# Constant products around the start of the attention, and the output stored in five transfers

## The chip, the cores and the metric

The kernel runs on one core of one Trainium2 chip. A core has four engines that compute: TensorE (PE in the profile) multiplies matrices into eight banks of 128 x 512 numbers, VectorE (DVE) and ScalarE (ACT) work elementwise, and GpSimd (POOL) here only issues gathers. SyncE (SP) issues transfers. Each engine runs its own list in order, and they wait for each other through semaphores. The metric is the device time of one execution in microseconds; less is better.

## What is computed

Two transformer layers on 512 rows of 1024 numbers, in 32-bit floats. What matters here are the attention of the first layer and the last product of the second:

```python
proj = jnp.einsum('bsd,de->bse', h, w_in)
(c_q, c_kv, k_r, q_b, k_b, v_b, q_i, k_i, w_i, g_a, g_b) = jnp.split(proj, splits, axis=-1)
...
o_a = chunk_causal_attention(q_a, k_a, v_a, (MLA_NOPE + MLA_ROPE) ** -0.5)
...
o_b = indexed_sparse_attention(q_b, k_b, v_b, q_i, k_i, w_i * (IDX_HEADS ** -0.5), top_k)
...
y = jax.nn.sigmoid(g_a) * y_a + jax.nn.sigmoid(g_b) * y_b
x = x + jnp.einsum('bsd,de->bse', y, w_out)
...
# second layer, its last stage: each row picks 128 of 16384 experts
act = jax.nn.gelu(jnp.einsum('chkd,cd->chk', u[ic], hc).astype(jnp.float32), approximate=False)
w = (gc * act).astype(h.dtype)
return jnp.einsum('chk,chkd->cd', w, v[ic])
```

Each of the two attentions has 8 heads and four blocks of 128 query rows; a block sees 512, 384, 256 or 128 keys. The sparse one masks all but the 128 best keys of a row, which a search with max and match_replace finds.

## The kernel before

The program is a row of blocks (`nc.Block()`). A block ends for all engines together: each goes on only when all have come to its end.

**The rows' stage** (the block of line 653) multiplies the normed rows with `w_in` in 40 pieces, each with a copy, a rotation and transposes behind it, and has the index search of the sparse attention beside it on VectorE (`dve_index`, lines 643 to 648). TensorE's list ends with a wait for the 24th index sum and `warm(e, 2, 7)` (line 706): two products of a constant matrix with a constant matrix into bank 7, which nobody reads. `warm` is the helper of lines 289 to 292; such products stand at eight more places of the program.

**The attention** (the block of line 825) runs two chains, `att_b` (sparse) and `att_a`, in steps, one head each a step, 32 heads and 7 more steps to drain. In step n TensorE does, for one chain and then for the other: the transposes of a finished block (line 401, few steps), the product of the weights with the values for head n - 5 (line 412, 64 columns each), the transposes of head n - 3 (line 421) and the product of queries and keys for head n (line 428). VectorE reduces that product (line 460), ScalarE takes the exponential (line 490), and the two take turns in copying the transposes (lines 451 and 481). The product for head n waits for the reduction of head n - 1 of its own chain, since both use the chain's one bank:

```python
if n:
    e.wait_ge(*(self.reduced if self.bias else self.powered)(n))
e.matmul(self.banks[0][:, 0:self.keys(i)], self.q(i, h), self.k(i, h), start=True, stop=True).then_inc(*self.scored.up(1))
```

The blocks with the most keys come first, so the first eight heads have 512 keys and the next eight 384. In the first three steps TensorE has nothing but the products of line 428. Bank 3, which belongs to chain b, is not used before the second block of query rows.

**The end** (the block of line 2512) multiplies gates with expert rows for row blocks 0 to 2 in 64 parts, `pe_second(e, n)`: part n is row group n // 2 and column half n % 2, and has for each row block `tb` twelve products into bank 2 * tb + n % 2 (lines 2505 to 2507). Each bank collects over all 32 groups. Row block 3 is worked out one row choice at a time by GpSimd's gathers and VectorE (`dve_row`, line 2153), the last of them at `r_used(256)`. When part 62 is done (`y_mm(63)`) VectorE adds the three banks of column half 0 to `X`, and when part 63 is done (`y_mm(64)`) those of column half 1 (line 2680). SyncE waits for the six additions and the row choices and stores all of `X` in one transfer (line 2554).

Of the kernel before, what the change touches and what calls it, by code (L numbers as in the profile page):

```python
# [175 lines left out]
def r(a):  # L176
    return a.bitcast(F32R)


def span(k, w=128):  # L180
    return slice(w * k, w * k + w)


def program(nc, d, out, sizes):
    ctx = ExitStack()
    with ctx:
# [4 lines left out]
        def sb2(name, shape, c):  # L191

            at = nc.sbuf_base
            a = sb(name, shape, c)
            assert at % 32 == 0 and nc.sbuf_base - at == 4 * int(np.prod(shape[1:]))
            t = nc.alloc_sbuf_tensor_at(name + "r", shape, F32, offset=at)
            return a, t[(slice(None),) * len(shape)]
# [3 lines left out]
        def sem(name, new=False):  # L201

            if new or not spare:
                s = Signal(ctx.enter_context(nc.semaphore(name)), 0)
            else:
                s = spare.pop(0)
            if not new:
                taken.append(s)
            return s
# [11 lines left out]
        X, XC = sb2("X", [128, 4, 1024], ctx)  # L221
# [31 lines left out]
        def wait_weight(e, n):  # L253
            e.wait_ge(*w_in[n % NS](16 * (n // NS) + 16))

        def weight(n):
            return W2[n % NS][0][:, 0:sizes[n]]
# [31 lines left out]
        def warm(e, times, bk, w=512):  # L289

            for _ in range(times):
                e.matmul(bank[bk][:, 0:w], ident, C[:, 0:w], start=True, stop=True)
# [207 lines left out]
        with ExitStack() as c0:  # L500
# [4 lines left out]
            with ExitStack() as c1:  # L505
                norm = Norm(c1, "mix", 0, 0, None, "mix")
                t_hi, t_lo = sems("t_hi t_lo")
                with nc.Block() as block:
                    @block.sync
                    def _(e):  # L510
                        e.dma_start(X, d["x"].rearrange("(b p) n -> p b n", p=128)).then_inc(*in_x.up(16))
                        e.dma_start(C, d["consts"]).then_inc(*in_c.up(16))
                        e.dma_start(G, d["gains"]).then_inc(*in_g.up(16))
                        load_weights(e, 3)
# [26 lines left out]
            with ExitStack() as c1:  # L541
# [111 lines left out]
                with nc.Block() as block:  # L653
# [4 lines left out]
                    @block.tensor  # L658
                    def _(e):
                        for step in range(45):  # L660
                            n = step
                            if n < 40:
                                t, tb = divmod(n, 4)
                                if tb == 0:
                                    wait_weight(e, t)
                                    if t in (6, 8):
                                        e.wait_ge(*r_keep(at[4 * (t - 6 if t == 6 else 5) + 3] + 1))
                                if n >= 2:
                                    e.wait_ge(*r_out(n - 1))
                                w, nw = weight(t), WIDTH[t]  # L670
                                bk = bank[n % 2][:, 0:nw]
                                if t < 6:
                                    hi, lo = RH[t % 2], W2[t % NS][1]
                                    for k in range(8):
                                        if tb == 0 and k % 2 == 0:
                                            e.wait_ge(*q_lo(4 * t + k // 2 + 1))
                                        a, c = span(tb), span(k, nw)
                                        e.matmul(bk, r(HTl[:, k, a]), r(hi[:, c]), start=k == 0, stop=False)
                                        e.matmul(bk, r(HTh[:, k, a]), r(lo[:, c]), start=False, stop=False)
                                        i = e.matmul(bk, r(HTh[:, k, a]), r(hi[:, c]), start=False, stop=k == 7)  # L680
                                else:
                                    lhs = cql if t < 8 else ckl
                                    for k in range(KK[t]):
                                        i = e.matmul(bk, lhs(k, tb), w[:, span(k, nw)], start=k == 0, stop=k == KK[t] - 1)
                                i.then_inc(*r_prod.up(1))
                            n = step - 4
                            if n in at:
                                t, tb = divmod(n, 4)
                                k = at[n]
                                e.wait_ge(*r_work(k + 1))  # L690
                                if k >= 2:
                                    e.wait_ge(*r_keep(k - 1))
                                s = SU[k % 4]
                                for g in range(2 if t == 8 else 1):
                                    bk = bank[2 + 2 * (k % 2) + g]
                                    p = 96 if t in (6, 7, 8) else 128
                                    srcs = [s[:, span(4 * g + j, p)] for j in range(2 if t == 5 else 4)]
                                    if t == 0:
                                        srcs[3] = kiN[:, tb, :]
                                    for j, x in enumerate(srcs):  # L700
                                        i = e.transpose(bk[0:p, span(j)], x, ident)
                                i.then_inc(*r_turn.up(1))
                            for u in index_units(step):
                                pe_logits(e, u)
                        e.wait_ge(*i_sum(24))
                        warm(e, 2, 7)

                    @block.scalar
                    def _(e):
# [115 lines left out]
                with nc.Block() as block:  # L825
                    @block.tensor
                    def _(e):
                        for step in range(att_b.steps()):
                            att_b.pe(e, step)
                            att_a.pe(e, step)  # L830

                    @block.vector
                    def _(e):
                        for step in range(att_b.steps()):
                            att_b.dve(e, step)
                            att_a.dve(e, step)

                    @block.scalar
                    def _(e):
                        for step in range(att_b.steps() + 1):  # L840
                            att_b.act(e, step)
                            att_a.act(e, step)
# [1233 lines left out]
        with ExitStack() as c0:  # L2076
# [90 lines left out]
            g_prod, g_hi, g_lo, v_hi, v_lo, y_mm, y_add = sems("g_prod g_hi g_lo v_hi v_lo y_mm y_add")  # L2167
# [51 lines left out]
            with ExitStack() as cx:  # L2219
# [247 lines left out]
                rows = lambda step: range(0 if step == 0 else round(turns[step - 1]), round(turns[step]))  # L2467
# [18 lines left out]
                    e.dma_start(AD[q // 4, :, q % 4, :], GA[q % 4]).then_inc(*ga_done[q % 4].up(16))  # L2486

                out_done = sem("out_done", True)

                def pe_second(e, n):  # L2490

                    g, c = n // 2, span(n % 2, 512)
                    gh, gl, vh, vl = GH[g % 2], GL[g % 2], VH[n % 3], VR[g % 2][1][:, :, c]
                    e.wait_ge(*g_lo(g + 1))
                    e.wait_ge(*v_lo(n + 1))
                    if n == 0:
                        e.wait_ge(*f_gelu(125))
                        e.wait_ge(*o_copy(96))
                    if n == 1:
                        e.wait_ge(*f_gelu(126))  # L2500
                        e.wait_ge(*c_ia(3))
                    for tb in range(3):
                        t, bk = span(tb), bank[2 * tb + n % 2]
                        for a in range(4):
                            e.matmul(bk, r(gl[:, a, t]), r(vh[:, a, :]), start=g == 0 and a == 0, stop=False)  # L2505
                            e.matmul(bk, r(gh[:, a, t]), r(vl[:, a, :]), start=False, stop=False)  # L2506
                            i = e.matmul(bk, r(gh[:, a, t]), r(vh[:, a, :]), start=False, stop=g == 31 and a == 3)  # L2507
                    i.then_inc(*y_mm.up(1))

                later = lambda n: range(ROWS1 + n * (256 - ROWS1) // 60, min(256, ROWS1 + (n + 1) * (256 - ROWS1) // 60))  # L2510

                with nc.Block() as block:
                    @block.sync
                    def _(e):
# [33 lines left out]
                        for k in range(2, 32):  # L2548
                            load_w(e, k)
                            load_a(e, k)  # L2550
                            load_v(e, k)
                        e.wait_ge(*y_add(6))
                        e.wait_ge(*r_used(256))
                        e.dma_start(out.rearrange("(b p) n -> p b n", p=128), X).then_inc(out_done.sem, 16)
                        e.wait_ge(out_done.sem, 16)

                    @block.gpsimd
                    def _(e):
# [71 lines left out]
                    def _(e):  # L2630
# [43 lines left out]
                            for q in later(n):  # L2674
                                dve_row(e, q)
                        for n in range(2):
                            e.wait_ge(*y_mm(63 + n))
                            for tb in range(3):
                                o = X[:, tb, span(n, 512)]
                                e.tensor_tensor(o, o, bank[2 * tb + n], ALU.add).then_inc(*y_add.up(1))  # L2680

# [16 lines left out]
```

## Time and profile before

| | us |
|---|---|
| median of 3 runs | 3118.2 |
| the runs | 3116.55, 3118.2, 3154.87 |
| device time of the profiled execution | 3154.56 |
| span of the profiled execution | 3152.7 |
| TensorE busy in it | 2977.3 (94%) |
| VectorE busy in it | 2002.0 (64%) |
| ScalarE busy in it | 1304.8 (41%) |
| mean granted TensorE clock, as a share of 2.4 GHz | 0.946 |

The span is the time from the first to the last instruction. The granted clock is what TensorE's throttle let through: 1.00 is 2.4 GHz and 0.50 is 1.2 GHz. A product of 32-bit numbers shows as two records. Matrix products are pipelined, and the end of a record is modelled: a record can reach into the next one, so the pace is read from start to start. Each row of a timeline merges like instructions that follow one another; "idle before" is the time in which that engine did nothing, with what released it.

### The profile page before, as it was taken

The page shows a single profiled execution, that of the slowest core. Times are in us where ns is not written, and L with a number is a line of the kernel's source. Part 1 is how long each engine was busy: PE and PEld are TensorE (multiplying, and loading weights), DVE is VectorE, ACT ScalarE, POOL GpSimd, SP SyncE. Part 2 cuts the span into 40 slices and gives each one's busy share as a digit, 9 for nine tenths or more (in the row PEclk, how much of TensorE's full clock was granted, in tenths as well). Part 3 has the DMA queues.
Part 4 walks back from the last instruction along what each step waited for, and adds up shares of the span by engine and source line. Part 5 has one row for each costly group of instructions (what it writes and reads, how often), then busy time and mean ns, then how long its engine had stood idle before and what let it go on. Part 6 is the DMA issues. An engine that isn't in the chain of part 4 may idle for free. (4 is left out here: it accounts for less than half of the span.)

```text
span 3152.7 us, 35761 instructions
## 1 busy us (share of the span) xinstructions
PE 2977.3 (94%) x13559; PEld 2369.0 (75%) x13559; DVE 2002.0 (64%) x3247; ACT 1304.8 (41%) x2107; POOL 407.1 (13%) x293
## 2 busy tenths in 40 slices
PE   7989999799999798989799999999999989999998
PEld 6756788578887345746566678999999987788887
DVE  4482433378887235634533248789898858888886
ACT  4332522267776222523321133336667643323332
POOL 0000000001000000000000000021111324545441
PEclk9995899799999898987699999999999999999999
DMA  4120062367677210120012233367777988999996
GB/s 166 38 76 6 1 154 102 154 229 291 263 293 277 81 60 27 67 74 29 1 57 97 78 114 111 117 237 247 263 273 275 352 332 310 384 391 388 388 389 241
DMA packets 159018, 585.93 MB, mean 186 GB/s; under 512 B 15104, under 2 KB 86400, under 8 KB 130560
## 3 DMA queue, kind: packets, MB, share of 16 engines
q1 hardware_dynamic: 100096, 421.59, 36.6%
q0 software_dynamic: 41472, 138.45, 11.8%
q10 hardware_dynamic: 17280, 23.60, 2.0%
q8 instruction: 109, 1.79, 0.2%
q14 instruction: 61, 0.50, 0.0%
HBM read 556.81 MB, written 64.52 MB: 197 GB/s over the span
## 5 line engine op out<-in xcount | busy, mean ns | idle before, releaser
L2139 POOL DMA_INDIRECT RG<-in_un,EI x128 | 178.8, 1397 | 1448.9 <-DVE EI L2391 1036.9
L2505 PE MATMUL bank<-VH,GL 128*128 128x512 f32 x768 | 301.9, 393 | 4.2 <-DVE VR1r L2217 2.1
L2507 PE MATMUL bank<-VH,GH 128*128 128x512 f32 x768 | 300.7, 392 | 0.0
L2139 POOL DMA_INDIRECT RG<-in_vn,EI x128 | 185.7, 1450 | 258.8 <-DVE X L2153 231.6
L2153 DVE SCALAR_TENSOR_TENSOR X<-RG,DG,X 128x1024 f32<-128x1024 f32 x128 | 164.1, 1282 | 44.1 <-DMA RG<-in_vn,EI 39.7
L2150 DVE CUSTOM_DVE_ANT_0 RG<-RG,HR 128x1024 f32<-128x1024 f32 x128 | 156.3, 1221 | 39.3 <-DMA RG<-in_un,EI 38.7
L2505 PEld LDWEIGHTS bank<-VH,GL 128*128 128x128 f32 x768 | 144.2, 188 | 41.5 <-issue 6.7
L2123 PE MATMUL bank<-HTl,UH1r 128*128 128x384 f32 x512 | 172.7, 337 | 0.0
L2124 PE MATMUL bank<-HTh,UH1r 128*128 128x384 f32 x512 | 172.6, 337 | 0.0
L2124 PE MATMUL bank<-HTh,UH0r 128*128 128x384 f32 x512 | 172.2, 336 | 0.0
L2123 PE MATMUL bank<-HTl,UH0r 128*128 128x384 f32 x512 | 172.1, 336 | 0.0
L2507 PEld LDWEIGHTS bank<-VH,GH 128*128 128x128 f32 x768 | 144.2, 188 | 32.5
L1737 PE MATMUL bank<-W,HT 128*128 128x384 f32 (+2 forms) x448 | 156.0, 504 | 1.4 <-ACT SV L1783 1.4
L2506 PE MATMUL bank<-VR0r,GH 128*128 128x512 f32 x384 | 152.7, 398 | 0.0
L2212 ACT ACTIVATE VH<-VR 128x2048 fp32r<-128x2048 f32 x64 | 119.2, 1908 | 79.9 <-DMA VR<-in_vn 79.9
L2506 PE MATMUL bank<-VR1r,GH 128*128 128x512 f32 x384 | 149.6, 390 | 0.0
L2428 ACT ACTIVATE OB<-OB,IA 128x128 f32<-128x128 f32 x384 | 122.3, 391 | 55.3 <-DVE OB L2421 54.8
L1737 PEld LDWEIGHTS bank<-W,HT 128*128 128x128 f32 x448 | 90.9, 220 | 62.2 <-issue 33.8
L2484 ACT ACTIVATE GA<-bank 128x384 f32<-128x384 f32 x120 | 58.3, 486 | 167.2 <-PE bank L2124 166.8
L940 PE MATMUL bank<-HTr,WH 128*128 128x512 f32 x320 | 125.4, 392 | 0.0
L2122 PE MATMUL bank<-HTh,UR0r 128*128 128x384 f32 x352 | 120.3, 342 | 1.0 <-DVE UR0r L2111 1.0
L2122 PE MATMUL bank<-HTh,UR1r 128*128 128x384 f32 x336 | 115.7, 344 | 4.2 <-DVE UR1r L2111 4.2
(597 smaller groups left out, 7537.3 us busy)
## 6 DMA issues: line engine op xcount, KB each, us to landing
UR<-in_u SPq DMA_DIRECT2D x64, 1024.0 KB, 6.7
VR<-in_vn SPq DMA_DIRECT2D x32, 2048.0 KB, 9.4
UP<-in_wup SPq DMA_DIRECT2D x22, 2048.0 KB, 7.9
DN<-in_wdn SPq DMA_DIRECT2D x32, 1024.0 KB, 7.2
W<-in_weights SPq DMA_DIRECT2D x20, 1536.0 KB, 7.0
W<-in_weights SPq DMA_DIRECT2D x14, 2048.0 KB, 8.3
wspill<-VR SPq DMA_DIRECT2D x12, 2048.0 KB, 8.7
aspill<-GA ACTq DMA_DIRECT2D x120, 192.0 KB, 5.4
```

Source lines behind the costliest of these rows:

```text
L940: e.matmul(bk, r(hi[:, k, span(b)]), r(HTl[:, k, :]), start=False, stop=False)
L1737: i = e.matmul(bank[4 + u % 2][:, 0:w], lhs(k), weight(t)[:, span(k, w)], start=k == 0, stop=k == 7)
L2122: e.matmul(bk, r(lo[:, k, :]), r(HH_[:, k, 0:NT3]), start=k == 0, stop=False)
L2123: e.matmul(bk, r(hi[:, k, :]), r(HL_[:, k, 0:NT3]), start=False, stop=False)
L2124: i = e.matmul(bk, r(hi[:, k, :]), r(HH_[:, k, 0:NT3]), start=False, stop=k == 7)
L2139: e.indirect_dma_start(RG[q % RR], None, d["un" if what == "u" else "vn"][:, :], off).then_inc(*row_in[q % RR].up(16))
L2150: e.tensor_tensor_reduce(RG[q % RR], RG[q % RR], HR3, 1.0, 0.0, ALU.mult, ALU.add, DT[:, s:s + 1]).then_inc(*r_used.up(1))
L2153: e.scalar_tensor_tensor(X[:, 3, :], RG[q % RR], DG[:, s:s + 1], X[:, 3, :], ALU.mult, ALU.add).then_inc(*r_used.up(1))
L2428: i = e.activation(OB[n % 3][:, j, :], OB[n % 3][:, j, :], ACT.Copy, scale=IA[:, 2, t:t + 1])
L2505: e.matmul(bk, r(gl[:, a, t]), r(vh[:, a, :]), start=g == 0 and a == 0, stop=False)
L2506: e.matmul(bk, r(gh[:, a, t]), r(vl[:, a, :]), start=False, stop=False)
L2507: i = e.matmul(bk, r(gh[:, a, t]), r(vh[:, a, :]), start=False, stop=g == 31 and a == 3)
```

## The change

It has two parts. TensorE gets eight more constant products: three more at the end of the rows' stage, and one in each of the attention's first five steps, between the work of chain b and that of chain a, into bank 3. And the end is cut finer: the last product of each row block in parts 62 and 63 raises a semaphore `y_sum` of its own, VectorE's six additions wait for these one by one, and `X` is stored in five transfers: row block 3, column half 0 of blocks 0 to 2, and column half 1 of blocks 0, 1 and 2 singly.

```diff
@@ the rows' stage, TensorE
                         e.wait_ge(*i_sum(24))
-                        warm(e, 2, 7)
+                        warm(e, 5, 7)
@@ the attention, TensorE
                         for step in range(att_b.steps()):
                             att_b.pe(e, step)
+                            if step < 5:
+                                warm(e, 1, 3)
                             att_a.pe(e, step)
@@ pe_second
                             i = e.matmul(bk, r(gh[:, a, t]), r(vh[:, a, :]), start=False, stop=g == 31 and a == 3)
-                    i.then_inc(*y_mm.up(1))
+                        if g == 31:
+                            i.then_inc(*y_sum.up(1))
+                    if g < 31:
+                        i.then_inc(*y_mm.up(1))
@@ the last block, SyncE
-                        e.wait_ge(*y_add(6))
+
+                        rows = out.rearrange("(b p) n -> p b n", p=128)
                         e.wait_ge(*r_used(256))
-                        e.dma_start(out.rearrange("(b p) n -> p b n", p=128), X).then_inc(out_done.sem, 16)
-                        e.wait_ge(out_done.sem, 16)
+                        e.dma_start(rows[:, 3, :], X[:, 3, :]).then_inc(out_done.sem, 16)
+                        e.wait_ge(*y_add(3))
+                        e.dma_start(rows[:, 0:3, 0:512], X[:, 0:3, 0:512]).then_inc(out_done.sem, 16)
+                        for tb in range(3):
+                            e.wait_ge(*y_add(4 + tb))
+                            e.dma_start(rows[:, tb, 512:1024], X[:, tb, 512:1024]).then_inc(out_done.sem, 16)
+                        e.wait_ge(out_done.sem, 80)
@@ the last block, VectorE
                         for n in range(2):
-                            e.wait_ge(*y_mm(63 + n))
                             for tb in range(3):
+                                e.wait_ge(*y_sum(3 * n + tb + 1))
                                 o = X[:, tb, span(n, 512)]
                                 e.tensor_tensor(o, o, bank[2 * tb + n], ALU.add).then_inc(*y_add.up(1))
```

TensorE's list at the border of the two stages and in the first steps of the attention, before (-) and after (+). L701 are the last transposes of the rows' stage, L292 is a constant product, L653 and L826 are the block's end and the next one's start, L428 the products of queries and keys (kbT for chain b, kaT for chain a) and L421 transposes:

```order
 L701 MATMUL bank<-C,SU 96x128 x8
-L292 MATMUL bank<-C 128x512 x2
+L292 MATMUL bank<-C 128x512 x5
 L653 UNCONDITIONAL_BRANCH
 L826 UNCONDITIONAL_BRANCH
 L428 MATMUL bank<-kbT,qbT 128x512
+L292 MATMUL bank<-C 128x512
 L428 MATMUL bank<-kaT,qaT 128x512
 L428 MATMUL bank<-kbT,qbT 128x512
+L292 MATMUL bank<-C 128x512
 L428 MATMUL bank<-kaT,qaT 128x512
```

Nothing is taken away or put in another order; a constant product comes in between b's product and a's.

SyncE's list at the end of the program, before, with the semaphores that each waits for as the program's numbering has them (a semaphore here bears the name that it had in an earlier stage; `r_keep` is `y_add`, `flippedb` is `r_used`):

```order
281 L2554 DMA out<-X 128x4x1024 [waits flippedb,r_keep]
282 L2512 UNCONDITIONAL_BRANCH [waits out_done]
```

And after:

```order
281 L2561 DMA out<-X 128x1024 [waits flippedb]
282 L2563 DMA out<-X 128x3x512 [waits r_keep]
283 L2566 DMA out<-X 128x512 [waits r_keep] x3
284 L2518 UNCONDITIONAL_BRANCH [waits out_done]
```

The one transfer of four row blocks has become five, of which the first no longer waits for the additions and only the last waits for the sixth.

## Rows read from the trace of the kernel before

**Rows 1.** The page: the span, and the clock digits in 40 slices.
```profile
span 3152.7 us, 35761 instructions
PEclk9995899799999898987699999999999999999999
```

**Rows 2.** Busy table: stretch, length, busy us (instructions) by engine, clock, DMA, GB/s.
```profile
237.00:238.00 1.00, 0.39 (x1) 0.42 (x2) 0.29 (x1) 0.42 (x1) 0.00 (x0) 0.73 0.44 184
238.00:239.00 1.00, 1.00 (x2) 0.08 (x1) 0.00 (x0) 0.86 (x1) 0.00 (x0) 0.50 0.00 0
...
237.60:329.60 92.00, 91.99 (x269) 58.46 (x269) 25.09 (x66) 27.38 (x64) 0.00 (x0) 0.50 0.00 1
330.60:380.00 49.40, 49.23 (x345) 40.22 (x345) 25.68 (x104) 29.04 (x100) 0.00 (x0) 1.00 0.01 1
1450.00:1490.00 40.00, 38.55 (x140) 28.36 (x139) 14.92 (x59) 16.78 (x62) 0.00 (x0) 0.57 0.07 28
1530.00:1575.00 45.00, 27.91 (x72) 15.32 (x72) 23.97 (x52) 9.04 (x25) 0.00 (x0) 0.54 0.00 0
```

**Rows 3.** Timeline, end of the rows' stage: start, length, engine, instruction, idle before.
```profile
232.85 1.88 PE L292 MATMUL bank<-C 128*128 128x512 f32 x4
...
236.86 0.43 DVE L648 TENSOR_SCALAR BI<-oTb 128x512 f32<-128x512 f32 x1
...
237.61 2.04 PE L428 MATMUL bank<-kbT,qbT 64*128 64x512 f32 x2 [2.88 <-PEq L653]
...
239.58 2.07 PE L428 MATMUL bank<-kaT,qaT 96*128 96x512 f32 x2
239.69 0.69 DVE L460 CUSTOM_DVE_ANT_0 Pb<-bank,BI 128x512 f32<-128x512 f32 x1 [2.40 <-PE bank L428]
```

**Rows 4.** Timeline of TensorE in the attention, single rows.
```profile
260.68 1.81 PE L412 MATMUL bank<-vb,cqT 128*128 128x64 f32 x8
...
317.95 1.49 PE L428 MATMUL bank<-kaT,qaT 96*128 96x384 f32 x2
...
325.58 1.49 PE L428 MATMUL bank<-kaT,qaT 96*128 96x384 f32 x2
...
329.67 0.91 PE L428 MATMUL bank<-kbT,qbT 64*128 64x384 f32 x2
...
331.95 0.81 PE L428 MATMUL bank<-kaT,qaT 96*128 96x384 f32 x2
...
334.48 0.88 PE L412 MATMUL bank<-va,cqT 128*128 128x64 f32 x6
...
335.54 0.81 PE L428 MATMUL bank<-kaT,qaT 96*128 96x384 f32 x2
...
376.72 0.43 PE L412 MATMUL bank<-va,cqT 128*128 128x64 f32 x2
```

**Rows 5.** Timeline, the end of the program.
```profile
3110.22 4.07 DVE L2153 SCALAR_TENSOR_TENSOR X<-RG,DG,X 128x1024 f32<-128x1024 f32 x3
...
3142.97 0.39 PE L2505 MATMUL bank<-VH,GL 128*128 128x512 f32 x1
...
3143.43 0.39 PE L2507 MATMUL bank<-VH,GH 128*128 128x512 f32 x1
3143.85 1.88 DVE L2680 TENSOR_TENSOR X<-X,bank 128x512 f32<-128x512 f32 x3 [6.27 <-PE bank L2507]
3145.76 0.39 SPq L2554 DMA_DIRECT2D out<-X  x1
```

**Rows 6.** DMA issues of the whole program: tensors, queue, count, KB each, median us to landing.
```profile
aspill<-GA ACTq DMA_DIRECT2D x120, 192.0 KB, 5.4
...
os<-XN SPq DMA_DIRECT2D x11, 512.0 KB, 2.6
...
out<-X SPq DMA_DIRECT2D x1, 2048.0 KB, 6.6
...
RG<-in_weights SPq DMA_DIRECT2D x8, 128.0 KB, 2.2
```

More of the change, by code:

```diff
@@ L2488, in program @@
                 out_done = sem("out_done", True)
+                y_sum = sem("y_sum", True)
                 def pe_second(e, n):
```

## The prediction

> **What bounds the kernel now.** I read the page first, then the busy table by stretches, then the engines' timeline at the two places that the diff touches, then the list of DMA issues.
>
> The page gives a span of 3152.7 us in the profiled execution, and its row of clock digits is mostly 9, with the exceptions 5, 7 and 6 [rows 1]. TensorE is the engine that is nearly always busy, so the places to look for are those where its clock is low and those where it is idle.
>
> The table by stretches shows what those digits hide. From 237.6 to 329.6 us TensorE is busy all the time (91.99 of 92.00 us) at a granted clock of 0.50, which is the lower level, 1.2 GHz. From 330.6 to 380 us, the same attention stage with the same kind of instructions, it is 1.00, the upper level, 2.4 GHz [rows 2]. The fall is between 237 and 238 us (0.73, then 0.50) [rows 2]. What TensorE did before it is in the timeline: it ended its two constant products at 234.73 and stood idle for 2.88 us, until the block's end let it go at 237.61. VectorE was the last there: its last operation of the rows' stage starts at 236.86 and takes 0.43 [rows 3]. Behind that gap the attention begins with products of 2.0 us each, start to start, and then keeps TensorE without idle time for 92 us, and still the clock doesn't rise until 329.67 [rows 3, 4]. So an engine that shows as busy is not enough to bring the clock back here, and a fall at this border is dear.
>
> The end of the program is a chain of three: TensorE's last product starts at 3143.43, VectorE then does three additions (1.88 us), SyncE issues one transfer of 2048 KB at 3145.76, which lands 6.6 us later [rows 5, 6].
>
> **The time of the profiled execution and the others.** Its device time is 3154.6, 1.9 over its span. The three runs are 3154.9, 3118.2 and 3116.6. So it agrees with the highest, and two others are 37.2 us shorter (mean 3117.4). No other stretch can hold 37 us of lost clock: the two next longest low stretches are 40 and 45 us at 0.57 and 0.54, and the second has TensorE busy for only 27.91 us [rows 2], so even a halving of all its busy time there gives under 20. I read the two shorter runs as runs in which the attention stage kept, or soon regained, 2.4 GHz. The change is then judged on two things: how often the fall happens after it, and what it costs or gives otherwise.
>
> **What the lower clock costs in this stage.** One step of 384 keys, from one product of kaT to the next, is 325.58 − 317.95 = 7.63 us at 0.50 and 335.54 − 331.95 = 3.59 us at 1.00 [rows 4]. The later step has six records of 64 columns for each head where the earlier has eight. Six of them last 0.88 us and two 0.43 [rows 4], so two more are (0.88 − 0.43) / 2 = 0.22 for each of the two heads; the like step is 3.59 + 0.44 = 4.03, and the ratio is 0.53. The 92.0 us at 0.50 become 92.0 × 0.53 = 48.8, and 43.2 us are saved where the fall doesn't come. The measured difference between the runs is 37.2. The 6 us between them are either my ratio (the first three steps, which are only products and reductions, may shorten less) or some 13 us at the low clock in the two short runs also.
>
> **Three more constant products at the border.** A constant product of 512 columns is two records; four records start at 232.85 and last 1.88, so one costs about 0.43 × 2 = 0.86 at the upper clock [rows 3]. Three add 2.57 us, from 234.73 to 237.30. VectorE ends at 236.86 + 0.43 = 237.29 and the block ends at 237.6 [rows 3]. So they lie almost wholly beside VectorE's search, and TensorE arrives as late as VectorE: nothing on the path if VectorE stays last, 0.3 if the block's end takes its 0.3 us again behind TensorE; I take 0.3. If VectorE were faster here, all 2.57 would be on the path. The gap of 2.88 shrinks to about 0.3.
>
> **One constant product in each of the first five steps.** It stands between the product for head b and that for head a. In steps 0 to 2 the next b product waits for VectorE's reduction of b (0.69, started right behind the product's end) [rows 3], which at the upper clock runs beside a's product. There is hardly a gap to fill there, so nearly all of 5 × 0.86 = 4.3 us is on the path; bounds are 0 (if waits of the same length stand there now) and 4.3, and I take 4.3. At the lower clock the price is double, 8.6. What is queued behind it on TensorE is head a's product, and VectorE's and ScalarE's work on head a waits for that; they come 0.86 later each step, which is this price and no other.
>
> The Trainium skill (TensorE: Matmul & The Clock Gate, Part 1) says that the array's clock is gated down when it has been idle and that sustained work releases it. The trace agrees: 0.50 right behind 2.88 us of idle time. The same page (Part 4) says that transposes don't count as work for this clock; by it the clock should fall again from the fourth step, where transposes start. The rows bear that out only in part: 330.6 to 380 us holds 1.00 with transposes in each step [rows 2].
>
> **The end.** The additions now start each when its row block's twelve products are done, 12 × 0.23 = 2.7 us apart (two records on start 0.46 later) [rows 5]. Behind the last product one addition is left instead of three: 1.88 − 0.63 = 1.25 us less. Behind it one transfer of 256 KB is left instead of 2048 KB. The trace has no such transfer; nearest are 128 KB in 2.2, 512 KB written to memory in 2.6, and on the dear side 192 KB in 5.4 under other traffic [rows 6]. Nothing else moves at the end, so I take 2.4, which saves 4.2, with bounds 1.2 and 4.4. Row block 3 can be stored when the last row's addition ends, at 3110.22 + 4.07 = 3114.3 [rows 5], the first half of the columns some 36 × 0.23 = 8.3 us ahead of the last product's end, and the next two blocks' transfers 5.4 and 2.7 us before the last, so four transfers are hidden behind products. SyncE issues each in 0.39 [rows 5] and has nothing else to do. Sum of the end: −5.5 (−2.5 to −5.7).
>
> The Trainium skill (DMA: Bandwidth & Descriptors, the cost components and the rules for authors) speaks against splitting: each transfer has a fixed 2.0 us beside its bytes at 436 GB/s, and small ones are to be merged. That fit gives 2.6 for the last transfer (an estimate), and the sum would be −5.3; the merging rule bites only if the five stood one behind the other.
>
> **Sum.** From the profiled execution: 3154.6 − 43.2 + 0.3 + 4.3 − 5.5 = 3110.5. From the two short runs, if they already held the clock throughout: 3117.4 + 0.3 + 4.3 − 5.5 = 3116.5. Both are the same case with the clock held; I have no row that decides between them and forecast 3113.
>
> **Rivals.**
> 1. *The clock is held (or regained in the first steps) and the end gets shorter.* 3113. For it: the gap goes from 2.88 to 0.3 us, and 50 us at 1.00 of the same stage. Chance 0.72.
> 2. *The last transfer is not cheap*: the ones before it are still under way, as the 192 KB transfers with 5.4 us to landing would be. The end then gives 2.5 and not 5.5: 3116. It is decided by whether a 256 KB transfer takes more than the 2.7 us between two. Chance 0.08; it lies in the same range.
> 3. *The clock falls again behind the fifth step*, when the constant products end and transposes and 64-column products fill the steps (the page's rule on transposes would do that). From 260.68 to 329.67 us [rows 4] 69.0 × 0.47 = 32.4 us come back: 3113 + 32 = 3145. Against it stand the 1.00 of 330.6 to 380 and the two short runs, which had no constant products and didn't lose the time. Chance 0.09.
> 4. *The other side: the fall comes all the same* in more than half of the executions, since the gap is not gone and SyncE's and ScalarE's share of the block end is unchanged. The stage then runs its 92 us as before and the constant products cost 8.6: 3154.6 + 8.6 + 0.3 − 5.5 = 3158, 40 us above the median of before. For it: 92 busy microseconds didn't raise the clock. It decides from the second low run in three. Chance 0.11.
>
> **Numbers.** Cases 1 and 2 hold 0.80. Their lower end is 3110.5 − 4.6 (constant products and border at nothing) − 1.6 (the distance of the two short runs) = 3104, their upper end 3116.5 + 3.0 (the dear transfer) + 1.6 = 3121, with one for rounding 3122. A change of about 2% (62 us) is what a measurement of this kernel can tell from none; no case reaches it in either direction (−14 to +40 us, and even against a before of 3155, 3113 is −1.3%). Within 2%: 0.98; 0.01 on each side for what I have not seen.
>
> **What would show it.** In the profile of the changed kernel: TensorE's idle time ahead of the first attention product under 0.6 us; a clock of 1.00 in the stage's first 50 us; first attention products of about 1 us instead of 2.04; a stage shorter by about 40 us than in the rows here; the last transfer landing about 2.4 us after its issue and the program ending about 3.3 us after the last product's end. Wrong would be: a clock of 0.50 anywhere in the stage; a median near 3118 with the end 5.5 shorter (the constant products then cost more than 4.6); or a last transfer above 4 us.

## The result, and the profile after

| | before | changed |
|---|---|---|
| median of 20 runs, us | 3130.18 | 3108.85 |
| lowest and highest, us | 3116.55, 3158.84 | 3099.66, 3118.94 |
| device time of the profiled execution, us | 3154.56 | 3110.66 |
| its span, us | 3152.7 | 3108.9 |
| its mean granted TensorE clock | 0.946 | 0.959 |

The ratio of the times is 0.9932, with a 95% interval of 0.9912 to 0.9952: 21 us less, clear of noise and under 2%. The scatter shrank as well, from 42 us to 19. The three runs shown ahead of the prediction had their median at 3118.2; with twenty it is 3130.2, so those three were two low ones and a high one. In the experiments below, a ratio is formed from the fast runs alone (two of the 35, and two of the 27, executions of the kernel before lie over 1.5% above its fastest and are left out of it), so it isn't the quotient of the two medians beside it.

The page of the changed kernel, span and clock digits. The digits at places 4 and 5 (236 to 394 us), low in [rows 1], are now 9.

```profile
span 3108.9 us, 35796 instructions
PEclk9999999799999998997699999999999999999999
```

The busy table by stretches for the changed kernel (columns as in [rows 2]):

```profile
237.00:238.00 1.00, 0.70 (x2) 0.29 (x2) 0.37 (x1) 0.34 (x1) 0.00 (x0) 1.00 0.50 209
238.00:239.00 1.00, 1.00 (x3) 0.28 (x2) 0.17 (x1) 0.95 (x1) 0.00 (x0) 1.00 0.00 0
237.60:329.60 92.00, 91.90 (x543) 64.80 (x543) 43.66 (x135) 48.86 (x133) 0.00 (x0) 1.00 0.00 1
```

The clock doesn't fall at the border. The 92 us of [rows 2] held 269 records of products at 0.50; a stretch of the same length and place now holds 543 at 1.00. TensorE shows as busy all the time in both, so the busy share says nothing of this difference; the count of instructions and the clock do.

The timeline of TensorE in the changed kernel, from the border on:

```profile
232.94 4.46 PE L292 MATMUL bank<-C 128*128 128x512 f32 x10
237.70 1.09 PE L428 MATMUL bank<-kbT,qbT 64*128 64x512 f32 x2 [0.30 <-PEq L653]
238.72 1.12 PE L292 MATMUL bank<-C 128*128 128x512 f32 x2
239.68 1.02 PE L428 MATMUL bank<-kaT,qaT 96*128 96x512 f32 x2
...
254.17 1.00 PE L412 MATMUL bank<-vb,cqT 128*128 128x64 f32 x8
...
290.49 0.91 PE L428 MATMUL bank<-kbT,qbT 64*128 64x384 f32 x2
```

The idle time at the border is 0.30 us and was 2.88 [rows 3]. The product at 290.49 is the one that stood at 329.67 [rows 4]; it comes 52.8 us after the attention's first, where it came 92.1 us after it.

The end of the changed kernel, in its timeline and its list of DMA issues:

```profile
3105.32 0.39 PE L2510 MATMUL bank<-VH,GH 128*128 128x512 f32 x1
3105.74 0.69 DVE L2692 TENSOR_TENSOR X<-X,bank 128x512 f32<-128x512 f32 x1 [2.03 <-PE bank L2510]
```

```profile
out<-X SPq DMA_DIRECT2D x1, 768.0 KB, 3.5
out<-X SPq DMA_DIRECT2D x3, 256.0 KB, 2.0
...
out<-X SPq DMA_DIRECT2D x1, 512.0 KB, 7.4
```

From the start of the first addition behind the last product to the end of the span it was 3152.7 − 3143.85 = 8.85 us [rows 1, 5] and is 3108.9 − 3105.74 = 3.16 us: 5.69 less.

### The profile page after: what moved, and what is told of

Same layout as the page of the kernel before. It is cut to its first block and busy times, and to the rows that moved or that the text cites. A ratio compares the mean times of both kernels' runs of the same rounds, so it can differ in the third digit from the quotient of the medians.

```text
span 3108.9 us, 35796 instructions
## 1 busy us (share of the span) xinstructions
PE 2943.8 (95%) x13575; PEld 2345.6 (75%) x13575; DVE 2002.4 (64%) x3247; ACT 1304.6 (42%) x2107; POOL 410.6 (13%) x293
## 5 line engine op out<-in xcount | busy, mean ns | idle before, releaser
L2155 DVE SCALAR_TENSOR_TENSOR X<-RG,DG,X 128x1024 f32<-128x1024 f32 x128 | 164.2, 1283 | 43.2 <-DMA RG<-in_vn,EI 38.9
```

Source lines behind the costliest of these rows:

```text
L2155: e.scalar_tensor_tensor(X[:, 3, :], RG[q % RR], DG[:, s:s + 1], X[:, 3, :], ALU.mult, ALU.add).then_inc(*r_used.up(1))
```

## The experiments

Four theories stood at the start. The border is the place between the rows' stage and the attention. (1) The idle time at the border lets the clock fall, and closing it brings the gain beside the 5.7 us of the end. (2) The five products in the steps hold or regain the clock. (3) The gain is all at the end and the rest is scatter. (4) The scatter comes from other stages.

### The end alone

```diff
-                        e.dma_start(out.rearrange("(b p) n -> p b n", p=128), X).then_inc(out_done.sem, 16)
+                        e.dma_start(rows[:, 3, :], X[:, 3, :]).then_inc(out_done.sem, 16)
...
-                            e.wait_ge(*y_mm(63 + n))
                             for tb in range(3):
+                                e.wait_ge(*y_sum(3 * n + tb + 1))
...
```

> Only the second part of the change: the six additions wait for their own products, and the output is stored in five transfers; the constant products are as before. My theory (the end is worth 5.7 us in every execution, and the rest of the gain is the clock at the start of the attention): median 5 to 7 us under that of the kernel before, and the same spread of some 40 us over the executions. Rival (the gain is all at the end, and the scatter of the executions is chance): the median falls by about 20 us, as in the whole change.

Measured: median 3118.6 of 12 runs (3109.5 to 3152.2); the kernel before beside it 3127.6 of 35. The medians are 9 us apart and the ratio is 1.0004 (0.9963 to 1.0045), so the times alone can't resolve 5 us in this scatter. Three of the twelve are at 3152, near the three highest of before (3153 to 3162). The profile resolves it: the last addition starts at 3116.89 and the span ends at 3120.0, 3.1 us. The end gives its 5.7 us and no more, and it leaves the scatter: (3) falls. In this profile the clock fell at the border also and came back after some 40 us:

```profile
239.00:278.00 39.00, 39.00 (x91) 19.98 (x91) 11.86 (x30) 12.80 (x31) 0.00 (x0) 0.50 0.00 0
279.00:290.00 11.00, 11.00 (x71) 7.90 (x69) 4.52 (x13) 5.44 (x13) 0.00 (x0) 1.00 0.00 1
```

### The border alone

```diff
-                        warm(e, 2, 7)
+                        warm(e, 5, 7)
```

> Only the three more constant products at the end of the rows' stage. Theory that the idle time of 2.9 us at the border decides: TensorE is idle for 0.3 us there, the attention runs at 1.00 in the profile, the median falls by 15 to 20 us (15.6 left after the end, and up to 4.3 more because the five products in the steps are not paid), and the highest executions of before disappear. Rival (the products in the steps hold or regain the clock): no gain at the median, highest executions near 3155 still there.

Measured: median 3106.3 of 12 (3100.6 to 3111.9), ratio 0.9924 (0.9896 to 0.9953). This one edit gives as much as the whole change (0.9932), and the least scatter so far, 11 us; what it lacks, the end with its 5.7 us and the five products in the steps with their 4.4 (both measured below), nearly cancel. Its profile shows 1.00 from 237.6 to 329.6 and 0.31 us of idle time at the border. Theory (1) holds.

### The five products in the steps alone

```diff
+                            if step < 5:
+                                warm(e, 1, 3)
```

> Only the five constant products in the attention's first five steps; the gap of 2.9 us at the border stays. Theory that the border decides: the clock falls as often as before, the stage pays 4.3 us (8.6 at the lower clock) more, median 4 us above before. Rival (these products bring the clock back within the first steps): the profile shows 0.50 at the stage's start and 1.00 before 260 us, the highest executions come down by some 35 us and the median by about 10.

Measured: median 3122.3 of 12 (3112.8 to 3127.6), ratio 0.9991 (0.996 to 1.0021). Both theories miss a part. The median is not above before, and the highest executions are gone, as (2) wants (18 of the 35 of before are above the highest here); but nothing is gained on the whole. The one profiled execution doesn't show how, because the clock didn't fall in it in spite of 2.9 us of idle time at the border:

```profile
236.24 1.09 PE L428 MATMUL bank<-kbT,qbT 64*128 64x512 f32 x2 [2.87 <-PEq L653]
237.26 1.13 PE L292 MATMUL bank<-C 128*128 128x512 f32 x2
```

So that gap makes the fall likely and not certain.

### The kernel before, once more

Nothing is edited.

> The kernel before, unchanged, for a second profiled execution of it. I read the shorter of its runs as runs whose attention kept 2.4 GHz. If so, a profile of a time under 3125 shows 1.00 from 237 to 330 us, and one near 3155 shows 0.50; one between them shows a part of the stage at 0.50. Rival (the scatter comes from other stages, above all 1400 to 1575 us): the time doesn't go with the clock of the stretch from 237 to 330 us.

Measured: median 3123.8 of 12 (3114.4 to 3137.8); the profiled execution has a span of 3115.9, so it is one of the short ones. The clock fell in it also, for some 13 us, and only at 240 us, when the attention's first products had run at 1.00 for over 2 us:

```profile
237.00:240.00 3.00, 2.15 (x5) 0.66 (x5) 1.19 (x4) 1.56 (x2) 0.00 (x0) 1.00 0.23 93
241.00:253.00 12.00, 12.00 (x20) 4.36 (x19) 3.50 (x10) 5.62 (x14) 0.00 (x0) 0.50 0.00 0
254.00:260.00 6.00, 6.00 (x34) 3.78 (x33) 3.55 (x10) 3.20 (x8) 0.00 (x0) 1.00 0.00 0
```

With the profiles of like code there is a scale. From the attention's first product to the next stage's first (line 939) it took 154.9 us with 92 us at 0.50 (the kernel before, [rows 2]), 128.1 us with 40 (the end alone), 121.4 us with 24 (only the additions, below), 115.2 us with 13 (this run), and 110.9 us with none (the border alone). That is 0.48, 0.43, 0.44 and 0.33 us lost for each microsecond at the low clock. The two profiles of the kernel before differ by 39.7 us inside this stretch and by 2.9 us outside it (3152.7 − 154.9 = 2997.8 and 3115.9 − 115.2 = 3000.7). The clock of the single executions says the same: of the 35 of before, those at 3106.6 and 3108.2 have a mean granted clock of 0.962 and 0.960, those between 3131 and 3140 one of 0.950 to 0.955, and those above 3150 one of 0.944 to 0.946. So (4) falls as the main cause.

For the 10 to 19 us of scatter that stay, the low stretches between 1400 and 1575 us are not the likely source: that window has a mean clock of 0.73 to 0.77 in all thirteen profiles. What does differ is a stretch near 532 to 556 us (23.2 us in the border alone and in this run, 26.4 in the kernel before and the changed one), one near 1005 to 1173 (167.6 us in the border alone, 171.0 in this run, in the kernel before and the changed one), and the last block, from its first product to its last: 535.3 us in the kernel before and 543.1 in the longest of the profiles, though the clock from 2620 to 3080 us is 1.00 in all thirteen. Why these differ is open.

### The end and the border, without the steps

```diff
                         for step in range(att_b.steps()):
                             att_b.pe(e, step)
-                            if step < 5:
-                                warm(e, 1, 3)
                             att_a.pe(e, step)
```

(against the changed kernel)

> The whole change without the five constant products in the steps. Theory (the gap at the border is what lets the clock fall, and the five products in the steps only cost): the attention at 1.00, 4.4 us less than the changed kernel, median near 3101 to 3104. Rival (the five products are needed in some executions to keep the clock): some executions 10 to 40 us above the others.

Measured: median 3101.6 of 10 (3096.5 to 3107.2), ratio 0.9917 (0.989 to 0.9945). It has the lowest median of this study, and no execution stands out. Against the changed kernel the medians are 7 us apart, but they are of different batches, and the intervals of the two ratios overlap (0.9912 to 0.9952 there), so the times alone don't prove the difference. The price of the five products can be read directly in the trace. Its timeline of TensorE:

```profile
232.74 4.46 PE L292 MATMUL bank<-C 128*128 128x512 f32 x10
...
237.50 1.09 PE L428 MATMUL bank<-kbT,qbT 64*128 64x512 f32 x2 [0.30 <-PEq L653]
...
249.58 1.00 PE L412 MATMUL bank<-vb,cqT 128*128 128x64 f32 x8
```

From the first product to the first of line 412 it is 12.08 us here and 254.17 − 237.70 = 16.47 us in the changed kernel: 4.39 us, all five on the path.

### No constant product at the border, without and with the five in the steps

```diff
                         e.wait_ge(*i_sum(24))
-                        warm(e, 2, 7)
```

> The kernel before with no constant product at the border, so that TensorE is idle for 2.9 + 1.7 = 4.6 us there. Theory (the idle time makes the clock fall): 0.50 from about 238 us in the profile and in nearly every execution; median 5 to 20 us above the kernel before. Rival (the length of the gap doesn't matter): as before.

> As the kernel without constant products at the border, but with the five in the attention's first steps. If these bring the clock back after a fall: 0.50 for at most about 15 us behind the border, no execution with a long low stretch, highest and lowest execution less than 20 us apart, median below that of the kernel without them in spite of their 4.4 to 8.6 us. If they don't: 5 to 9 us above it and the same scatter.

Measured: without the five, median 3126.8 of 10 (3120.3 to 3137.3), ratio 0.9996 (0.9969 to 1.0023); with them 3120.9 of 10 (3112.0 to 3126.6), ratio 0.9978 (0.995 to 1.0006). The first forecast missed at the median: 4.6 us of idle time cost no more than 2.9. None of the ten executions is below 3120.3, where six of the 27 of before are, and none is above 3137.3, where three of before are; ten runs are few for either. The fall came in both profiles. Without the five the clock stayed low for some 41 us:

```profile
239.00:278.00 39.00, 39.00 (x91) 19.84 (x90) 11.34 (x30) 13.38 (x31) 0.00 (x0) 0.50 0.00 0
280.00:290.00 10.00, 10.00 (x64) 7.36 (x64) 4.08 (x12) 5.12 (x13) 0.00 (x0) 1.00 0.01 2
```

With the five it was back after some 7:

```profile
235.00:236.00 1.00, 0.00 (x0) 0.00 (x0) 0.93 (x4) 0.00 (x0) 0.00 (x0) 0.88 0.97 406
236.00:242.00 6.00, 5.25 (x6) 1.67 (x6) 1.12 (x3) 2.10 (x3) 0.00 (x0) 0.50 0.11 44
243.00:253.00 10.00, 10.00 (x31) 4.30 (x30) 4.35 (x15) 5.91 (x14) 0.00 (x0) 1.00 0.00 0
```

So theory (2) is probably right about what the five do behind a fall: they cut the low stretch short, for 4.4 us in every execution. One profile of each shows it, and the kernel before came back after 13 us without them, so the profiles alone don't decide; but none of the 22 executions with the five and an open border is above 3127.56, and 18 of the 35 and 17 of the 27 of before are. A gain at the median is not shown: the intervals of 0.9978 and 0.9996 overlap, and that of 0.9991 (the steps alone) holds 1. Where the border is closed there is nothing to cut short.

### Of the end, only the additions

```diff
-                            e.wait_ge(*y_mm(63 + n))
                             for tb in range(3):
+                                e.wait_ge(*y_sum(3 * n + tb + 1))
```

> Of the end only the additions that wait one by one; the output in one transfer. From the start of the last product to the end of the span it was 9.27 us before and 3.58 with the whole change. Expected here: 9.27 - 1.2 = 8.1 us, which leaves 4.5 to the smaller last transfer. Rival (the single transfer starts no earlier, because something else holds it): 9.3.

Measured in its timeline and its DMA issues (span 3129.0):

```profile
3121.36 0.69 DVE L2684 TENSOR_TENSOR X<-X,bank 128x512 f32<-128x512 f32 x1 [2.03 <-PE bank L2508]
3122.08 0.39 SPq L2558 DMA_DIRECT2D out<-X  x1
```

```profile
out<-X SPq DMA_DIRECT2D x1, 2048.0 KB, 6.6
```

From the last addition's start to the end it is 3129.0 − 3121.36 = 7.64 us, against 8.85 before and 3.16 with the whole change: 1.21 us belong to the additions and 4.48 to the smaller last transfer. Counted from the last product's start, as the expectation has it, that is 8.1 of 9.27.

### How much of the gap must be closed

```diff
-                        warm(e, 5, 7)
+                        warm(e, 3, 7)
```

(against the kernel with end and border; likewise with 4 and 8)

> The end as changed, nothing in the steps, three constant products at the border, so that 2.0 us of idle time are left there (it was 2.9 with two and 0.3 with five). If any shortening of the gap helps in proportion: median some 3110, between the 3118.6 of the kernel with two and the 3101.6 of the one with five. If only a closed gap helps: near 3118, with the same wide scatter.

> As before this, with four products at the border and 1.2 us of idle time left. In proportion: median near 3105. Only a closed gap helps: near 3118. A short gap is as good as a closed one: near 3101, with executions less than 15 us apart.

> Eight products at the border: three more than are hidden beside the search on the vector engine. The clock stays at 1.00 in the attention, and the stage begins 3 x 0.86 = 2.6 us later: median 3104. If the surplus is hidden after all: 3101.6 as with five.

| constant products at the border | idle time there, us | median, us | lowest, highest | runs |
|---|---|---|---|---|
| 3 | 2.0 | 3104.7 | 3099.9, 3129.6 | 10 |
| 4 | 1.2 | 3105.7 | 3097.3, 3129.6 | 10 |
| 5 | 0.3 | 3101.6 | 3096.5, 3107.2 | 10 |
| 8 | 0.3 | 3110.7 | 3106.2, 3120.5 | 10 |

With three and four most executions are as short as with five, but two of ten and one of ten are over 3120 (3122.3, 3129.6; 3129.6). Their profiles are of short executions and show 1.00 throughout the stage. The high ones have no profile, but their mean granted clock is on record: 0.953 and 0.954 for the two at 3129.6, against 0.958 to 0.962 for those under 3115. The kernel with no constant product at the border had 0.954 at 3131.3, with its 41 us at the low clock. So a fall at the border is the likely cause. Neither proportion nor "only a closed gap helps" is right: a shorter gap makes the fall rarer. Each product both shortens the idle time and lengthens TensorE's work ahead of it, and no run changes one without the other; which of the two holds the clock is not separated.

Eight products begin the attention 2.6 us later, as expected (TensorE's first attention product is at 239.40, 7.33 us after the first constant product, against 4.76 with five), but the median is 9 us higher and not 2.6. The traces show that the rest is not lost at the border. The two profiled executions are 12.2 us apart (spans of 3108.6 and 3096.4), and the next stage begins within 0.3 us of the same time in both:

```profile
348.07 0.51 PE L939 MATMUL bank<-Xr,W1r 128*128 128x512 f32 x1
```

(with eight)

```profile
348.40 0.79 PE L939 MATMUL bank<-Xr,W1r 128*128 128x512 f32 x1
```

(with five). The 2.6 us were paid, but with five the clock fell at the attention's end, which is told below, and with eight it didn't: from the attention's first product to the next stage's first it is 110.9 us with five and 108.7 with eight. From there to the last block's first product it took 2218.6 us with eight and 2208.7 with five, and the last block 2.7 us more. Of the 9.9 us, 3.1 and 3.4 lie in the two stretches near 532 and 1005 us that were named above; the changed kernel, with five products, is as long in both as this one. So a surplus at the border isn't shown to cost 9 us; what sets those later stretches stays open.

## Why the prediction was right, point by point

- **The fall at the border and what it costs.** Right. The ratio of 0.53 gave 48.8 us for the 92; the changed kernel's 52.8 us less its 4.4 us of constant products are 48.4.
- **The two short runs.** Of the two readings, "kept" or "soon regained" 2.4 GHz, the second was right where it could be seen: some 13 us at the low clock in an execution with a span of 3115.9. That is the figure that the difference of 6 us had pointed to, though it is another execution than the two short ones, which have no profile. But the prediction took two kinds of execution for what is a range: low stretches of 13, 24 and 92 us were seen with TensorE's list of the kernel before (and 40 with the end alone), and the median over more runs lies at 3130 between them. The sum that started from 3117.4 therefore started from runs that were short, and the other one, from the profiled execution, was the sound one: it said 3110.5, and the changed kernel's profiled execution took 3110.7. The terms agree about as well: from the attention's first product to the next stage's first it is 154.86 us before and 115.75 after, 39.1 less where −43.2 + 4.3 gives 38.9, and the end 5.7 for 5.5. An agreement within 0.2 us is luck all the same, since the rest of the program, outside that stretch, differs by 2.9 us between two executions of the kernel before.
- **Three more products at the border.** Taken as 0.3 us on the path, they cost nothing at the border: from the first constant product to the attention's first product it is 237.61 − 232.85 = 4.76 us before [rows 3] and 237.70 − 232.94 = 4.76 after. VectorE's search covers them exactly, and no more than these: with eight the attention began 2.6 us later.
- **Five products in the steps.** Taken as 4.3 us, measured 4.4. What the prediction did not ask is whether they are needed beside the closed border. They are not: without them no execution stood out, and the attention's first steps took 4.4 us less.
- **The end.** Taken as 5.5, measured 5.69: 1.21 for the additions (1.25 forecast) and 4.48 for the transfer (4.2). The 256 KB landed in 2.0 us, under the row of 128 KB in 2.2 [rows 6]; the value of 2.4 was too dear. The fit in the Trainium skill (DMA: Bandwidth & Descriptors, Anatomy of one DMA), 2.0 us and the bytes at 436 GB/s, gives 2.6 us for it as an estimate; it was 2.0 here, and the measurement decides. The page states this fit for transfers that GpSimd issues, and SyncE issued these, which the prediction left out. The early transfer of 512 KB took 7.4 us and cost nothing, since it lies under products.
- **Rival 2, a dear last transfer.** It landed in 2.0 us, under the 2.7 between two of them.
- **Rival 3, a second fall behind the fifth step.** None of the profiles with a closed or shortened gap shows it up to 329.6 us, though transposes stand in each step from the fourth on. The Trainium skill (TensorE: Matmul & The Clock Gate, Part 4) says that transposes don't count as TensorE's work in the same way; as a reason to expect a fall here it isn't borne out, as the stage has 1.00 with them. What the changed kernel does show is a fall where the attention ends, as the kernel before has it there too (0.50 from 385 to 391 us):

```profile
344.02 0.66 PE L401 MATMUL bank<-C,ckvT 128*128 128x128 f32 x4 [0.87 <-DVE ckvT L442]
344.92 0.66 PE L401 MATMUL bank<-C,ckvT 128*128 128x128 f32 x4 [0.25 <-DVE ckvT L442]
346.52 7.49 PE L292 MATMUL bank<-C 128*128 128x512 f32 x10 [0.94 <-PEq L825]
```

```profile
346.00:352.00 6.00, 5.48 (x7) 2.41 (x8) 3.56 (x3) 5.72 (x5) 0.31 (x1) 0.50 0.01 3
```

It begins in the stage's last microsecond, so the sign "a clock of 0.50 anywhere in the stage" was too wide: it appeared, and doesn't speak against the mechanism. With eight products at the border the same idle times of 0.87, 0.25 and 0.94 us were followed by no fall.

- **Rival 4, the fall all the same.** The one profile has none, and none of the twenty runs is above 3118.9, 39 us under the 3158 of this rival. A short fall, cut off by the five products, can't be told from these times alone; but the 22 executions with a closed border and no products in the steps are all at 3111.9 or less.

So forecast, range and direction held. The forecast of 3113, between two sums, was 4 us above the median for the reason above. For the same reason the gain was undersized: 5 us against the median of the first three runs, where twenty runs of each give 21. That the range held anyway rests on the sum from the profiled execution.

## What to carry to other kernels

Where a stage's end leaves TensorE idle while another engine finishes, count the idle time and fill it with constant products up to that engine's end. Up to there they were free here, and with five of them the clock held at the border in every profile, and some 20 us and most of the scatter went; those beyond it only begin the next stage later. Products put into the stage's own steps are on the path: here they cost 4.4 us and, with the border open, took only the highest executions away and no measured time off the median. When an execution's profile agrees with the highest of a few runs, take more runs or profile again before choosing which of them the sum starts from.

## What the runs showed of the hardware that was not expected

- A TensorE that showed as busy for 100% of a stretch stayed at 1.2 GHz for 13, 24, 40 or 92 us, with the same instructions of TensorE in the same order; what ended these stretches was not found. In the one profile with a constant product of 512 columns in each step and a fall, it ended after some 7 us.
- The same idle time of 2.9 us was followed by a fall in four profiled executions (the kernel before twice, the end alone, the additions alone) and by none in a fifth (the steps alone); 4.6 us were followed by one in both, 2.0, 1.2 and 0.3 us by none in any, though times of executions without a profile point to falls behind 2.0 and 1.2. One fall came 2 us after the idle time had ended, behind products at 1.00. At the attention's end idle times of 0.87, 0.25 and 0.94 us were followed by a fall in the changed kernel and by none with eight products at the border.
- A store of 256 KB landed in 2.0 us, and one of 2048 KB in 6.6.
